# One program for the latent projections and the attention, with head 0 loaded early, other score banks and a one-product fold of the outputs

## What is computed

```python
q = (rmsnorm(c_q, g_q[l]) @ w_uq[l]).reshape(b, s, MLA_HEADS, MLA_QK)        # 8 heads, 64 + 32 wide
q_nope, q_pe = q[..., :MLA_NOPE], apply_rope(q[..., MLA_NOPE:], cos, sin)
kv = (rmsnorm(c_kv, g_kv[l]) @ w_ukv[l]).reshape(b, s, MLA_HEADS, MLA_NOPE + MLA_V)
k_nope, v = kv[..., :MLA_NOPE], kv[..., MLA_NOPE:]
...
sc = jnp.einsum('bhqd,bhkd->bhqk', qi, k).astype(jnp.float32) * scale
mask = key_chunk[None, :] <= qc[:, None]                                     # chunks of 64 frames
sc = jnp.where(mask, sc, -jnp.inf)
p = jax.nn.softmax(sc, axis=-1).astype(v.dtype)
return jnp.einsum('bhqk,bhkd->bhqd', p, v)
```

## Time and profile before

| | us |
|---|---|
| median of 3 runs | 2475.88 |
| lowest, highest | 2471.88, 2479.92 |
| the profiled execution, its own time | 2472.47 |
| its span, first to last instruction | 2470.5 |
| TensorE (PE) busy | 2224.6, 90% |
| VectorE (DVE) busy | 1059.1, 43% |
| ScalarE (ACT) busy | 919.2, 37% |
| GpSimd (POOL) busy | 327.7, 13% |

### The profile page before, as it was taken

The page is one execution under the profiler, slowest core; times in us unless marked ns, Lnnn a source line. Parts: engine busy times, 40 slices in busy tenths (PEclk is TensorE's granted clock), DMA queues, the critical chain, the costliest instruction groups (busy, mean ns, idle before and its releaser), DMA issues. The chain is left out here.

```text
span 2470.5 us, 33500 instructions
## 1 busy us (share of the span) xinstructions
PE 2224.6 (90%) x11536; PEld 1847.4 (75%) x11536; DVE 1059.1 (43%) x1874; ACT 919.2 (37%) x1715; POOL 327.7 (13%) x222
## 2 busy tenths in 40 slices
PE   6999999999979999999678849888989884899998
PEld 5888888777868888888556737777777773788887
DVE  6000000000024444444365517777777674664653
ACT  7111111001034444444353216556556563543541
POOL 1222214214011111111022210000000000300000
PEclk9999999999989999999879868999999996999999
DMA  5222222223023332332474470223212305764752
GB/s 180 77 75 70 69 75 61 94 85 127 34 68 96 95 93 93 93 94 85 159 233 157 150 173 23 67 66 68 55 34 51 69 7 171 218 197 143 212 162 68
DMA packets 212449, 256.32 MB, mean 104 GB/s; under 512 B 38945, under 2 KB 137889, under 8 KB 208673
## 3 DMA queue, kind: packets, MB, share of 16 engines
q1 hardware_dynamic: 187616, 208.31, 29.6%
q10 hardware_dynamic: 23616, 43.00, 4.6%
q0 software_dynamic: 1152, 4.19, 0.5%
HBM read 157.41 MB, written 98.04 MB: 103 GB/s over the span
## 5 line engine op out<-in xcount | busy, mean ns | idle before, releaser
L1728 ACT ACTIVATE pT<-turn 128x512 fp32r<-128x512 f32 (+1 forms) x320 | 158.5, 532 | 201.4 <-PE turn L1855 200.8
L1785 DVE TENSOR_TENSOR pT<-turn,pT 128x512 fp32r<-128x512 f32 (+1 forms) x320 | 184.2, 607 | 92.6 <-ACT pT L1728 92.4
L66 PE MATMUL bankD<-hT_hi,shared_w_hi 128*128 128x512 f32 x512 | 212.3, 415 | 11.7 <-POOLq L676 11.7
L66 PE MATMUL bankA<-hT_hi,shared_w_hi 128*128 128x512 f32 x544 | 212.7, 391 | 0.0
L68 PE MATMUL bankA<-hT_hi,shared_w_lo 128*128 128x512 f32 x544 | 211.9, 390 | 0.0
L67 PE MATMUL bankA<-hT_lo,shared_w_hi 128*128 128x512 f32 x544 | 211.9, 389 | 0.0
L1771 DVE TENSOR_REDUCE chunk_min<-scores 128x1 f32<-128x512 f32 (+2 forms) x320 | 184.4, 607 | 60.8 <-PE scores L1841 38.6
L68 PE MATMUL bankD<-hT_hi,shared_w_lo 128*128 128x512 f32 x512 | 201.7, 394 | 0.0
L67 PE MATMUL bankD<-hT_lo,shared_w_hi 128*128 128x512 f32 x512 | 200.9, 392 | 0.0
L66 PE MATMUL scores<-k_sb,q_sb 96*128 96x512 f32 (+2 forms) x320 | 131.5, 411 | 76.2 <-ACT probs L1718 37.9
L1718 ACT ACTIVATE probs<-scores,least 128x1024 f32<-128x1024 f32 (+2 forms) x192 | 167.1, 870 | 39.9 <-DVE least L1778 39.1
(11 more groups left out here) (233 smaller groups left out, 4553.6 us busy)
## 6 DMA issues: line engine op xcount, KB each, us to landing
projT<-stage ACTq DMA_DIRECT2D x68, 256.0 KB, 2.4
shared_w_raw<-in_w_in_dram SPq DMA_DIRECT2D x32, 512.0 KB, 4.4
projT<-d_stage ACTq DMA_DIRECT2D x64, 256.0 KB, 2.4
e_l_in<-projT SPq DMA_DIRECT2D x64, 256.0 KB, 4.7
gateTok<-stage ACTq DMA_DIRECT2D x32, 256.0 KB, 2.0
shared_w_lo<-hgTok SPq DMA_DIRECT2D x16, 512.0 KB, 3.4
knT<-b_out SPq DMA_DIRECT2D x32, 256.0 KB, 2.8
vTok<-b_out SPq DMA_DIRECT2D x32, 256.0 KB, 3.0
```

The source lines that it names most:

```text
L66: pe.matmul(out, a_hi, b_hi, start=first, stop=False)
L1728: act.activation(pT[:, at % RING, 0, r0 * P:], turn[:, TURN_AT[tile] % 3, r0 * P:], ACT.Copy)\
L1785: dve.tensor_tensor(pT[:, at % RING, 1, r0 * P:], turn[:, TURN_AT[tile] % 3, r0 * P:], pT[:, at % RING, 0, r0 * P:].bitcast(F32), ALU.subt ...
```

## The change

- `latent_projections` and `attention` become parts of one program on each engine (`latent_and_attention`) without the barrier and the clearing between them. A few small tensors (`Small`) are shared; the large ones of the attention lie over those of the projections in another order, so that head 0's buffers lie over weights that are no longer read. The mask constants and the first counts of semaphores are set before the projections.
- Head 0's keys, shared key and queries are loaded from within the query projections: keys and values behind the store of (Q, 1, 1), the shared key behind (Q, 1, 4), queries a block at a time behind the last store of blocks 1, 2 and 3, and those of the last block when all is stored. Head 1 is loaded behind them.
- The first scores wait for `const_in` (two transfers of the new constant `fold`, issued behind the last queries), for the last reads of the projections' PSUM banks (`banks_read`), and for the first keys and queries.
- `LED` becomes 9, so row 8 is made ahead too; tiles per step are given by `TILES_AT`; rows 8 to 11 go round the four banks (`3 * r`), and a row whose first bank is bank 3 has a first piece of one chunk (`chunks_of`).
- In a step in which a block ends, TensorE does its values ahead of the transposes, and ScalarE copies `o_acc` ahead of `hi_part`. With four tiles in a step, the fourth is turned behind the values.
- The outputs are turned and their halves added by one fp32 product with `fold` (two identities of 64 above each other, 64 columns) in place of each transpose, L1754 and L1798 go, and the sums are inverted a step earlier.

The diff, cut to its core (the projections' functions are otherwise only indented anew):

```diff
+        def banks_read(pe):
+
+            pe.wait_ge(turned_ready, turn_use(Q, NB - 1, Q_EV - 1) + 1)
+            pe.wait_ge(rs_ready, len(NORMS))
+            pe.wait_ge(std_ready, len(NORMS))
...
+            def stored_up_to(n):
+
+                for slot, s in enumerate(stored):
+                    sp.wait_ge(s, 32 * ((n - slot + OUTS - 1) // OUTS))
...
+                    if g == Q and blk > 0 and i == X_AT + 1:
+                        stored_up_to(number(Q, blk, X_AT))
+                        attend.load_first_queries(sp, blk - 1)
+                    if (g, blk, i) == (Q, 1, 1):
+                        sp.wait_ge(w_ready, len(W_PARTS))
+                        sp.wait_ge(prod_done, Q_FIRST)
+                        stored_up_to(Q_FIRST)
+                        attend.load_first_keys(sp)
+                    if (g, blk, i) == (Q, 1, X_AT):
+                        sp.wait_ge(k_stored, 16 * 4 * NB)
+                        attend.load_first_shared_key(sp)
...
+            stored_up_to(E_END)
+            attend.load_first_queries(sp, NB - 1)
...
 AHEAD = 2
-LED = 2 * TPB
+TURN_RING = 3
+LED = 2 * TPB + 1
 
 
 def attention_schedule():
 
-
-
-    def tiles(*blocks):
-        return [(b, j) for b in blocks for j in range(TPB * (b + 1))]
-
-    def dealt(some, n):
-        return [some[i * len(some) // n:(i + 1) * len(some) // n] for i in range(n)]
-
-    steps = [[LED + r, some, None, None] for r, some in enumerate(dealt(tiles(0, 1), TPB) + dealt(tiles(2), TPB))]
-    steps += [[r, some, None, None] for r, some in enumerate(dealt(tiles(3), LED))]
+    TILES_AT = {9: 4, 10: 3, 11: 3, 12: 4, 13: 3, 14: 3, 15: 4,
+                0: 0, 1: 0, 2: 1, 3: 2, 4: 2, 5: 2, 6: 2, 7: 3, 8: 4}
+    tiles = [(b, j) for b in range(NB) for j in range(TPB * (b + 1))]
+    steps = []
...
-        return c + (r if b == 0 else 2 * (r % 2) if b == 1 else 0)
+        return (c + (r if b == 0 else 2 * (r % 2) if b == 1 else 3 * r if b == 2 else 0)) % 4
+
+    def chunks_of(i, piece):
+
+        b = i // TPB
+        cut = min(1 if s_bank(i, 0) == 3 else 2, b + 1)
+        return (0, cut) if piece == 0 else (cut, b + 1)
...
+        def load_first_keys(sp):
+            for part in range(2):
+                sp.dma_start(k_sb[0][0:NOPE, part].bitcast(F32), knT[0, part, 0:NOPE]).then_inc(first_k, 16)
+            sp.dma_start(v_sb[0][:].bitcast(F32), vTok[0]).then_inc(first_v, 16)
+
+        def load_first_shared_key(sp):
+            for part in range(2):
+                sp.dma_start(k_sb[0][PE_ROWS, part].bitcast(F32), kpT[part]).then_inc(first_k, 16)
+
+        def load_first_queries(sp, blk):
+            cols = slice(blk * BLK, (blk + 1) * BLK)
+            for part in range(2):
+                sp.dma_start(q_sb[0][0:NOPE, part, cols].bitcast(F32), qnT[0, part, 0:NOPE, cols]).then_inc(first_q[blk], 16)
+                for y in range(2):
+                    sp.dma_start(q_sb[0][NOPE + y * (ROPE // 2):NOPE + (y + 1) * (ROPE // 2), part, cols].bitcast(F32),
+                                 qpT[part, y, 0:ROPE // 2, cols]).then_inc(first_q[blk], 16)
...
+        def sync(sp):
+            for half in range(2):
+                sp.dma_start(fold[half * VD:(half + 1) * VD, :], ident_d[0:VD, 0:VD]).then_inc(const_in, 16)
+            for part in range(2):
+                sp.dma_start(k_sb[1][PE_ROWS, part].bitcast(F32), kpT[part]).then_inc(head_in[1], 16)
...
+            load_head(0, 1)
+            with sp.Fori(0, PAIRS - 1) as i:
+                for u in range(2):
+                    store_head(i, u)
+                    sp.wait_ge(head_done, i * 2 + (u + 1))
+                    load_head(i + 1, u)
...
+            act.wait_ge(latent.k_stored, 16 * 4 * NB)
+
+            def head(h, more):
+                for i, tiles, done, o_block in STEPS:
+                    row_of = h + 1 if i is not None and i < LED else h
+                    if done is not None:
+                        act.wait_ge(pv_done, h * TILES + (TILE_AT[done, TPB * (done + 1) - 1] + RING + 2))
+                        if done > 0:
+                            act.wait_ge(turned, h * TURNS + (TURN_AT["o", done - 1] + 1))
+                        act.activation(oT[:], o_acc[:], ACT.Copy).then_inc(o_copied, 1)
+                    for tile in tiles[:AHEAD]:
+                        hi_part(h, tile)
+                    if i is not None and (more or i >= LED):
+                        exponentials(row_of, i, 0)
+                    for tile in tiles[AHEAD:]:
+                        hi_part(h, tile)
+                    if i is not None and i >= 2 * TPB and (more or i >= LED):
+                        exponentials(row_of, i, 1)
...
+            def outputs(h, b):
+                at = TURN_AT["o", b]
+                n = h * NB + (b + 1)
+                dve.wait_ge(inv_ready, n)
+                dve.wait_ge(turned, h * TURNS + (at + 1))
+                dve.wait_ge(o_stored[b % 2], h * 32 + (b // 2 * 16 + 16))
+                dve.tensor_tensor(o_out[:, b % 2], turn[at % TURN_RING][:, 0:TPB * VD].rearrange("p (t n) -> p t n", n=VD),
+                                  inv[:].unsqueeze(2).to_broadcast([P, TPB, VD]), ALU.mult).then_inc(o_ready, 1)
+                dve.wait_ge(o_ready, n)
+                dve.sem_inc(turn_read, 1)
...
+            pe.wait_ge(const_in, 32)
+            pe.wait_ge(const_set, 2)
+            latent.banks_read(pe)
+            pe.wait_ge(first_k, 64)
...
+                    if not tiles:
                         for tile in before:
                             values(h, tile, u)
+                        before = []
...
+                    if i is not None and i >= LED:
+                        queries(h, i, u)
+                    elif i is not None and more:
+                        if i == 0:
+                            if u == 0:
+                                pe.wait_ge(head_in[1], pair * 144 + (144 + 32))
+                            else:
+                                pe.wait_ge(head_in[0], pair * 144 + 144)
+                        queries(h + 1, i, 1 - u)
+                    for tile in before:
+                        if tile[0] == done:
+                            values(h, tile, u)
+                    for tile in tiles[:TURN_RING]:
+                        transposes(h, tile)
+                    for tile in before:
+                        if tile[0] != done:
+                            values(h, tile, u)
+                    for tile in tiles[TURN_RING:]:
+                        transposes(h, tile)
+                    before = tiles
+                    if o_block is not None:
+                        at = TURN_AT["o", o_block]
+                        pe.wait_ge(o_copied, h * NB + (o_block + 2))
+                        pe.wait_ge(turn_read, h * TURNS + (at - 1))
+                        for r in range(TPB):
+                            last = pe.matmul(turn[at % TURN_RING][:, r * VD:(r + 1) * VD], oT[:, r * P:(r + 1) * P], fold[:], start=r == 0,
+                                             stop=r == TPB - 1, skip_group_check=True)
+                        last.then_inc(turned, 1)
+                        if o_block == NB - 1:
+                            pe.wait_ge(turned, h * TURNS + TURNS)
+                            pe.sem_inc(head_done, 1)
+
+            for i in range(LED):
+                if i % TPB == 0:
+                    pe.wait_ge(first_q[i // TPB], 96)
+                queries(0, i, 0)
+            pe.wait_ge(first_q[NB - 1], 96)
+            pe.wait_ge(first_v, 16)
```

More of the change, by code:

```diff
@@ new lines, in gpsimd, with split_out @@
+        def gpsimd(pool):
+            pool.memset(eps[:], EPS).then_inc(const_set, 1)
+            pool.memset(ones[:], 1.0).then_inc(const_set, 1)
+            def split_out(g, blk, i):
+                e, use = number(g, blk, i), turn_use(g, blk, i)
+                pool.wait_ge(out_hi, use + 1)
+                pool.tensor_tensor(out[:, e % OUTS, 1], turned[:, use % TURNED], out[:, e % OUTS, 0].bitcast(F32), ALU.subtract)\
+                    .then_inc(out_lo, 1)
+            for g, blk in BLOCKS:
+                for i in range(V_AT if g == KV else Q_EV):
+                    split_out(g, blk, i)
@@ L1807, in _ @@
+            if dve is not None:
                 dve.sem_inc(turn_read, 1)
@@ L1809, in _ @@
                     dve.sem_inc(s, 16)
-                def head(h, more):
-                    for i, tiles, _, o_block in STEPS:
-                        if i is not None and (more or i >= LED):
-                            minima(h + 1 if i < LED else h, i)
-                        for tile in tiles:
-                            lo_part(h, tile)
-                        if o_block is not None:
-                            outputs(h, o_block)
-                for i in range(LED):
-                    minima(0, i)
@@ new lines, in scalar, with exponentials, hi_part @@
+        def scalar(act):
+            def exponentials(h, i, piece):
+                b, r = i // TPB, i % TPB
```

(27 more changed lines are left out.)

1124 lines of the change are left out of this document (532 added, 592 removed).

## The result

The changed kernel takes 2438.0 us (median of 4 runs, 2432.8 to 2443.7) against 2475.6 us for the kernel before on the same chip: a ratio of 0.9848 with a 95% interval of 0.9821 to 0.9875. In a second set it was 2438.1 against 2473.1, 0.9862 (0.9845 to 0.9878). The forecast was 2433, its range 2416 to 2456. The profiled execution took 2443.7 (span 2441.9), the slowest of the four.

The account below looks back on a forecast made before the run. TensorE, busy 2224.6 of 2470.5 us, was taken as the bound, so gains come from its idle time, clock or work. Terms -20 - 5 - 21 + 2.6 = -43.4 gave 2429 for the profiled execution, 2433 as median; range 2416 to 2456.

Parts of the forecast that it names:

- The seam, -20: Between projections and attention: barriers go, head 0 loads early, first scores at about 1452 against 1472.2; -20 us.
- Cost for the query projections, 0: Query blocks 1 to 3: added loads and issues in SyncE's queue cost 0, up to +10 for the range.
- First rows of head 0, -5: Start of attention: wait of 1.34 goes, nine transposes move, less half clock worth 1.5; -5 us.
- last head, +2.6: Last head: last 16 tiles at VectorE's pace start about 3 us later, final chain 0.4 shorter; +2.6 us.
- The waits of a head, -2.5: Head loop: TensorE's idle waits sum to 5.3 us against 7.8, -2.5 a head.
- The fold, +1.65 a head: Head loop: fp32 products with `fold` take 0.81 a block, +0.41 for each of four blocks, +1.65 a head.
- four passes: Rival, heads' output turning: each fp32 product takes four full passes with own loads, +26, 2459 us; chance 0.04.
- Half-clock stretches, -2.1 a head: Head loop: one half-clock stretch every second head in place of two a head, 1.4 each; -2.1 a head.
- Seven passes, -3.0 a head: Head loop: waits, fold and half-clock stretches together -3.0 a head, times 7, -21 us.
- Stretches stay: Rival, heads: half-clock stretches remain, a head gains 0.85, 15 us back, 2448 us; chance 0.20.
- Seam half back: Rival, seam: loads and issues delay query projections or `fold` lands late, +10, 2443 us; chance 0.10.
- better: Rival, whole kernel: no half-clock stretches, earlier scores, fold at 0.4; 2419 us; chance 0.10.

Follow-up runs that it names:

- the second execution: The changed kernel profiled and timed again, nothing changed: 2438.1 us (2435.2 to 2440.2).
- The seam alone: Changed kernel's one program and early loads of head 0, but the attention of the kernel before: 2457.6 us against 2476.1, ratio 0.9919.
- The open hole of 2.9 us: Changed kernel with `fold` loaded at the start of the projections and a fetch hint on TensorE's head loop: 2417.8 us.
- the filled one: Changed kernel with `fold` loaded early, fetch hint on TensorE's head loop, and twelve unused products between last projection product and first scores: 2414.4 us.
- the fold early: Changed kernel with the two transfers of `fold` moved to the start of the latent projections: 2424.1 us; with a fetch hint on TensorE's head loop too: 2417.8.
- the hint: Changed kernel with an instruction-fetch hint on the jump back of TensorE's head loop: 2432.1 us (2428.5 to 2434.4).
- The old banks: Changed kernel with `fold` loaded early and fetch hint on TensorE's head loop, but the score banks and pieces as before: 2429.6 us.
- the filling: Six unused products a head in two TensorE waits, added to the kernel with early `fold`, fetch hint and filled seam hole: 2406.3 us, ratio 0.9728.
- one edit of SyncE's queue: Changed kernel with `fold` loaded early (2424.1 us), or with head 0's keys and values behind query block 3's inputs (2434.0 us).
- a loop with as many instructions: Changed kernel with outputs turned as before and each block's four transposes run twice, no fp32 product, no hint: 2451.4 us (2446.1 to 2457.5).

## Why the prediction held, step by step

- **The seam, -20: right.** First scores 15.6 us behind the last product and ended by `fold`, as written; queue and mechanism were read from the earlier trace rows. The first scores start at 1457.24 and in the second execution at 1451.91 (forecast 1452, bounds 1450 and 1460): the projections ended 5 later in the first, where `fold` so landed behind 1456, one of the forecast's signs of being wrong, though the queue behind the last product took as long as forecast. The seam alone measured -18.5.
- **Cost for the query projections, 0: low by 1 to 3 in most executions, within the +10 kept for the range.** In the second execution the last product starts 0.5 to 0.7 ahead of the kernel before. But in nine of eleven traces with these loads ScalarE waits 2.2 to 3.2 us for block 3's inputs, and TensorE's last wait in these blocks grows from 4.7 to 5.7 or more. The forecast looked at the slack of the result slots and not at the loads of inputs in the same queue. "The query blocks grow" was another of its signs of being wrong. The rest of the 1441.24 of the first profile was difference between executions, 2.3 of it ahead of the query blocks.
- **First rows of head 0, -5, and last head, +2.6: missed by 2 to 5 together.** From the first scores to the end of the attention, less the seven periods, it was 83.3 and 82.3 before and is 83.2 and 85.1. The wait of 1.34 went, but the part for the clock had the wrong sign: half clock stayed for 23.5 and 28.9 us behind the first scores in two executions, where it had been 19.2. I took its length to follow from the idle time ahead. The open hole of 2.9 us and the filled one showed that a hole of that length is enough to begin it and that a shorter hole ends it no sooner (22 and 28 us behind the first scores in two kernels with the fold early). ScalarE's load of its table, 1.28 us ahead of the first exponential, stood in the idle stretch between the stages before and stands in the open now.
- **The waits of a head, -2.5: right in place, better in size.** 0.4 to 0.95 ahead of the fourth transpose (1.2 forecast), 0.79 in row 11's scores (1.0), 0.17 in row 13's (0.35), 0.58 in row 14's (0.7), 0.77 at the fold and 0.3 at the values in the head's end (1.4). Each is shorter than walked: with the hint TensorE is idle for 23.3 of 400 us in the heads (1560 to 1960), 4.0 a head, where it was 43.4, 7.7 a head: -3.7. The old banks' +1.3 a head shows how much of this is the rotation.
- **The fold, +1.65 a head: slightly low.** From the first of its eight records to the next product it takes 0.91 (1488.94 to 1489.85) in most places and 0.81 in some, so +0.4 to +0.5 a block, up to +2.0 a head. The 1.6 a block of four passes did not come. The Trainium skill (FP8 and Floating Point Precision, TensorE Precision Notes) counts four passes; the trace shows two records and 0.23 us for each product, and how many passes stand behind a record no run shows. What the forecast missed is on the other side: L1754 and L1798 were put at nothing because their engines have room. In the new order they are waited for: with them back, TensorE waits 20 us longer for VectorE in seven heads.
- **Half-clock stretches, -2.1 a head: the direction right, the size too large.** Two lengths of 3.4 a head before (13 in all); with the hint six, nearly one a head where I counted one in two. "Waits of 0.7 have none behind them" failed: two of them 5 us apart do, as the filling shows. Seven lengths fewer in seven heads are, at 1.4 each, -1.4 a head and not -2.1. Removing six lengths together with two waits shortened the period by 1.2, 8.7 us in seven heads with the filling's cost in it, so one is worth about 1.4 in these two profiles, as forecast (0.8 to 1.4 by the ratios and the medians of the times).
- **Seven passes, -3.0 a head: right for a period, save the jump back.** With the hint a period is 68.1 (476.5 in seven) against 71.3 (498.3 and 499.5), -3.2. Without it, 481.2 and 485.2. That -3.0 and -3.2 lie so close is in part luck: the waits came out 1.2 better, the clock 0.7 and the fold up to 0.35 worse than in the sum.
- **What no step of the sum had: instruction fetch, +5 to +9.** I counted the fold's time on TensorE and not what it does to the loop's fetching. It is as large as what separates 2433 from 2438: with the hint the kernel takes 2432.1. The forecast of the whole held by its two large terms, the seam and the heads; that the rest of it stayed within 5 us is in part luck too, for the heads gave 1 to 2 more than the sum says and the first rows of head 0, the last head and the query projections less.
- **Rivals.** "Stretches stay" came true by half, on top of the fetches. "Seam half back", "four passes" and "slower" did not show; "better" needed edits that the change does not have.

## What to carry to other kernels

After two stages are joined, read what the first instruction of the second still waits for: here two small transfers of a constant behind twelve others cost 14 us, which moving them gave back. When a TensorE loop changes, look at the instruction packets of the page and at waits named "issue" at the jump back before trusting a sum of durations. A hole of 3 us in front of a full stretch cost as much again by the clock, and unused products in a wait are a cheap way to see how much (filling it gave 3.4 to 5).

## What the runs showed that was not expected

- Nine instruction packets and a wait of 3.9 to 4.4 us (0.7 to 0.9 without a miss) for each jump back that misses, and the miss comes and goes between executions (twice and once in two profiles of the changed kernel; once and twice in the two with one edit of SyncE's queue). Each miss has an instruction packet 1.2 to 2.9 us ahead of the jump, and no other jump has. Why `fold` brings it, and a loop with as many instructions does not in the one profile of it, stays open.
- A pass of TensorE's head loop before is 736 products, 736 weight loads and 194 other instructions, 1666 in all, and it was not fetched again between 1620 and 1900 us. The Trainium skill (Advanced Engine Details and Errata, ISA Cache) gives TensorE 128KB and lines of 16KB or 256 instructions; that makes eight lines, an estimate from these figures, and the trace agrees, for 1666 instructions are 6.5 lines. The same section's "Only 2 cache lines!" does not hold for TensorE here. The changed loop, with 1733 instructions or 6.8 lines, was fetched again all the same, so its number of instructions against that room does not explain the misses.
- A hole of 2.9 us put TensorE at half clock for 20 us in which it was 97% busy (18.75 of 19.40), and behind holes of 2.9 to 16 us the half clock stood for 22 to 29 us from the first scores on in the kernels with the new order, for 19 in the one with the old; within heads a length of half clock is 3.4 us, and up to four follow one another behind a jump back that misses.
